# The last expert's down product by column halves: output sums in interleaved quarters

## The reference

```
h2 = rmsnorm(x, ffn_norm_w)
# for each token its top 4 of 32 experts, gates = softmax of their logits
u = h2[tokens of e] @ w_up[e] + b_up[e]          # 1024 -> 2048
glu = min(u[:, 0::2], 7);  lin = clip(u[:, 1::2], -7, 7)
a = glu * sigmoid(1.702 * glu) * (lin + 1)
y = a @ w_down[e] + b_down[e]                    # 1024 -> 1024
x[tokens of e] += gate * y
```

## Time and profile before

| | |
|---|---|
| median of 3 runs | 1147.87 us |
| the three runs | 1146.83, 1147.87, 1149.91 us |
| span of the profiled execution | 1145.4 us |
| TensorE busy | 1097.6 us (96%) |
| VectorE, ScalarE, GpSimd busy | 437.5, 188.0, 88.4 us |
| HBM read, written | 439.78 MB, 2.37 MB |
| mean DMA rate over the span | 386 GB/s |

### The profile page before, as it was taken

The page is one execution under the profiler, slowest core; times in us unless marked ns, Lnnn a source line. Parts: engine busy times, 40 slices in busy tenths (PEclk is TensorE's granted clock), DMA queues, the critical chain, the costliest instruction groups (busy, mean ns, idle before and its releaser), DMA issues.

```text
span 1145.4 us, 15065 instructions
## 1 busy us (share of the span) xinstructions
PE 1097.6 (96%) x6055; PEld 497.1 (43%) x6055; DVE 437.5 (38%) x858; ACT 188.0 (16%) x398; POOL 88.4 (8%) x161
## 2 busy tenths in 40 slices
PE   9999999999999999999898999999999999999997
PEld 6689898543333333333333333333333333333332
DVE  4577786753433223233223232323232323232322
ACT  2133341221321101010101010101010101010101
POOL 1785215000000000000000000000000000000000
PEclk9999999999999999999999999999999999999999
DMA  9947629999999999999999999999999999999997
GB/s 313 314 128 186 210 85 353 416 357 425 400 420 426 419 432 431 430 433 431 433 433 429 434 430 433 435 428 434 429 434 431 431 434 429 435 429 434 425 423 287
DMA packets 53206, 444.36 MB, mean 388 GB/s; under 512 B 13101, under 2 KB 19373, under 8 KB 35741
## 3 DMA queue, kind: packets, MB, share of 16 engines
q1 hardware_dynamic: 46712, 435.83, 91.7%
q0 software_dynamic: 5600, 7.32, 2.4%
q10 hardware_dynamic: 852, 0.64, 0.2%
HBM read 439.78 MB, written 2.37 MB: 386 GB/s over the span
## 4 chain that ended last, share of the span: by engine, by line
PE 62%; DMA 37%; DVE 0%; issue 0%; ACT 0%; ACTq 0%; SPq 0%; DVEq 0%
PE pA L2051 32%; PE pB L2051 21%; DMA ring<-in_w_up 21%; DMA ring<-in_w_down 10%; PE pM L2051 6%; DMA area<-in_w_up 5%; PE pM L2054 1%; PE pA L2054 1%; DMA x<-in_x_prompt 1%; ACT area L1269 0%; DVE x L1898 0%; SPq L800 0%; DVE conv_row L1812 0%; DVE area L1973 0%; DVE x L1978 0%
## 5 line engine op out<-in xcount | busy, mean ns | idle before, releaser
L2051 PE MATMUL pA<-ring,hn 128*64 128x512 f32 x1536 | 352.6, 602 | 23.0 <-DMA ring<-in_w_up 23.0
L2051 PEld LDWEIGHTS pA<-ring,hn 128*64 128x64 f32 x1536 | 105.3, 137 | 218.8 <-issue 185.5
L2051 PE MATMUL pB<-ring,area 128*64 128x512 f32 (+2 forms) x784 | 171.5, 591 | 6.6 <-DMA ring<-in_w_down 5.8
L2051 PE MATMUL pA<-area,hn 128*64 128x512 f32 x512 | 119.3, 610 | 10.4 <-DMA area<-in_w_up 10.4
L2051 PE MATMUL pB<-area,ring 128*128 128x132 f32 (+2 forms) x928 | 126.4, 327 | 0.0
L2051 PEld LDWEIGHTS pB<-area,ring 128*128 128x128 f32 (+1 forms) x928 | 106.7, 175 | 18.2 <-issue 2.3
L2051 PEld LDWEIGHTS pB<-ring,area 128*64 128x64 f32 (+2 forms) x784 | 58.5, 136 | 101.2 <-issue 87.8
L1898 DVE TENSOR_TENSOR x<-pM,x 128x512 f32<-128x512 f32 x60 | 40.1, 691 | 147.7 <-PE pM L2051 147.7
L1257 ACT ACTIVATE area<-area 128x512 f32<-128x512 f32 x30 | 18.9, 631 | 385.2 <-DVE area L1881 385.2
L1812 DVE COPY conv_row<-pM 128x512 f32<-128x512 f32 x30 | 20.6, 686 | 146.0 <-PE pM L2051 146.0
L2051 PEld LDWEIGHTS pA<-area,hn 128*64 128x64 f32 x512 | 36.2, 139 | 74.5 <-issue 59.7
(11 more groups left out here) (348 smaller groups left out, 907.1 us busy)
## 6 DMA issues: line engine op xcount, KB each, us to landing
ring<-in_w_up SPq DMA_DIRECT2D x36, 4096.0 KB, 29.8
ring<-in_w_down SPq DMA_DIRECT2D x18, 4096.0 KB, 29.0
area<-in_w_up SPq DMA_DIRECT2D x12, 4096.0 KB, 30.2
ring<-in_w_up SPq DMA_DIRECT2D x16, 2048.0 KB, 13.4
area<-in_w_down SPq DMA_DIRECT2D x6, 4096.0 KB, 30.0
ring<-in_w_in SPq DMA_DIRECT2D x22, 1024.0 KB, 10.0
ring<-in_w_down SPq DMA_DIRECT2D x16, 1024.0 KB, 11.6
ring<-in_w_up SPq DMA_DIRECT2D x16, 1024.0 KB, 8.4
```

Source lines behind the costliest of these rows:

```text
L2051: return pe.matmul(out, w, m, start=start, stop=stop, skip_group_check=True)
```

## The change

Only the last pair is changed. The four quarters of the 1024 output columns (256 each) are dealt out anew: a = 0 makes quarters 0 and 2, a = 1 quarters 1 and 3. For expert 1 every product of 512 columns becomes two of 256, so that columns 0 to 511 (half 0) collect in one place and columns 512 to 1023 (half 1) in another bank (`last_down`). The last weight row comes in two loads of 512 columns, and half 0 of that row is multiplied as soon as the first is there. `half_done` then lets ScalarE and VectorE copy half 0, and `last_scatter` has a list of six products for each half. The sums of the prompt rows lie so that an addition of VectorE covers two quarters that are not neighbours; the last two stores follow suit. The bias of half 1 is added later, by `last_bias(1)` behind up piece 6. The diff, cut to its core:

```
+        def last_down(a, h):
+            rows_ = slice(64 - 64 * a, 128 - 64 * a)
+            return pA[rows_, 512:768] if h else pB[rows_, 1, 0:256]
+        def last_sums(m, a):
+            if m:
+                return pA[:, 1024 + 512 * a:1536 + 512 * a]
+            return pB[:, 0, :] if a else pA[:, 0:512]
...
+                        if j == 11 and r == ROWS:
+                            cut = SLOT * h + D * (ROWS - 1) + 512
+                            first_half = slice(cut - 512, cut)
+                            sp.dma_start(unit(u)[:, first_half], rows_of(b, PAIRS - 1)[:, first_half]).then_inc(last_half, 16)
+                            f = slice(cut, cut + 512)
...
-                    nc.scalar.activation(y_pair[64:128, 0:512], pB[64:128, 1, :], ACT.Copy).then_inc(y_ready, 1)
+                    act.wait_ge(half_done, 1)
+                    nc.scalar.activation(y_pair[64:128, 0:256], last_down(0, 0), ACT.Copy).then_inc(half_act, 1)
+                    act.wait_ge(down_done, 2 * g + 2)
+                    nc.scalar.activation(y_pair[64:128, 512:768], last_down(0, 1), ACT.Copy).then_inc(y_ready, 1)
...
+                        dve.wait_ge(half_done, 1)
+                        V.tensor_copy(y_pair[0:64, 256:512], last_down(1, 0)).then_inc(half_dve, 1)
                         dve.wait_ge(down_done, 2 * g + 2)
-                        V.tensor_copy(y_pair[0:64, 512:1024], pB[0:64, 1, :]).then_inc(y_ready_dve, 1)
+                        V.tensor_copy(y_pair[0:64, 768:1024], last_down(1, 1)).then_inc(y_ready_dve, 1)
...
+                        if last and (j, r) == (11, ROWS - 1):
+                            for n in range(2):
+                                if n == 0:
+                                    pe.wait_ge(last_half, 16)
+                                else:
+                                    loaded(j, whole=True)
+                                for a in range(2):
+                                    f = slice(D * r + 512 * n + 256 * a, D * r + 512 * n + 256 * a + 256)
+                                    mm = matmul(last_down(a, n), rows_T[:, r, 64 * h:64 * h + 64], w[:, f], start=False)
+                                if n == 0:
+                                    mm.then_inc(half_done, 1)
+                            continue
...
                         for a in range(2):
+                            if last and e == 1:
+                                for n in range(2):
+                                    mm = matmul(last_down(a, n), rows_T[:, r, 64 * h:64 * h + 64],
+                                                w_r[:, 512 * n + 256 * a:512 * n + 256 * a + 256], start=False, stop=False)
...
                 def last_scatter():
+                    for h in range(2):
+                        pe.wait_ge((half_act, y_ready)[h], 1 + g * h)
+                        pe.wait_ge((half_dve, y_ready_dve)[h], 1 + g * h)
+                        for m in (1, 0):
+                            for a in range(2):
+                                rows_ = slice(64 - 64 * a, 128 - 64 * a) if m else slice(0, 128)
+                                f = slice(512 * h + 256 * a, 512 * h + 256 * a + 256)
+                                mm = matmul(last_sums(m, a)[:, 256 * h:256 * h + 256], gate_h[a][rows_, 128 * m:128 * m + 128],
+                                            y_pair[rows_, f], start=(m == 0 and h == 0), stop=(h == 1))
+                                if h:
+                                    mm.then_inc(last_full, 1)
+                        for q in (2 * h, 2 * h + 1):
+                            mm = matmul(b[32 * q:32 * q + 32, 0:256], gate_h[q % 2][:, SEQ:], y_pair[:, 256 * q:256 * q + 256])
                     mm.then_inc(misc_full, 1)
```

More of the change, by code:

```diff
@@ L929, in _ @@
             sp.dma_start(y_prompt[0, 128:256, :], x[:, 1, :]).then_inc(final_stored, 16)
[L930 to L933, removed]
+            for a in range(2):
+                sp.wait_ge(last_dve, 2 + a)
+                sp.dma_start(quarters_of(y_prompt[0, 0:128, :], a), quarters_of(x[:, 0, :], a)).then_inc(final_stored, 16)
             sp.wait_ge(misc_free, MAIN_FILLS)
@@ L2569, in biases, with last_bias @@
                         up_biases(e)
+                    if last and e == 1:
+                        last_bias(0)
+                        return
                     for a in range(2):
+                        if last:
+                            matmul(in_two(pB[y_rows(e, a), e, :]), sel[0:96, e, :],
+                                   quarters_of(bias_down[0:96], a), stop=False)
+                            continue
                         matmul(pB[y_rows(e, a), e, :], sel[0:96, e, :], bias_down[0:96, 512 * a:512 * a + 512],
                                stop=False)
+                def last_bias(h):
+                    for a in range(2):
+                        f = slice(512 * h + 256 * a, 512 * h + 256 * a + 256)
+                        matmul(last_down(a, h), sel[0:96, 1, :], bias_down[0:96, f], stop=False)
                 def act_turn(e, freed=False):
@@ L2599, in down @@
                             w_r = first_down(j, r) if first else w[:, D * r:D * r + D]
+                            if last and e == 1:
+                                for n in range(2):
+                                    mm = matmul(last_down(a, n), rows_T[:, r, 64 * h:64 * h + 64],
+                                                w_r[:, 512 * n + 256 * a:512 * n + 256 * a + 256], start=False, stop=False)
+                                    if freed and r == a == n == 0:
+                                        mm.then_inc(ring_free, 1)
+                                continue
+                            if last:
+                                mm = matmul(in_two(pB[y_rows(e, a), e, :]),
+                                            rows_T[:, r, 64 * h:64 * h + 64], quarters_of(w_r, a),
+                                            start=False, stop=(h == 1 and r == ROWS - 1))
+                                continue
                             mm = matmul(pB[y_rows(e, a), e, :], rows_T[:, r, 64 * h:64 * h + 64], w_r[:, 512 * a:512 * a + 512],
@@ L2661, in first_expert_sums @@
                     pe.wait_ge(y_first, 1)
[L2662 to L2666, removed]
+                    for a in range(2):
+                        s = slice(64 * a, 64 * a + 64)
+                        matmul(in_two(last_sums(1, a)), gate_h[a][s, 128:256], quarters_of(y_pair[s], a),
+                               start=(a == 0), stop=False)
@@ L2668, in last_scatter @@
                 def last_scatter():
                     b = bank(6)
-                    pe.wait_ge(y_ready, g + 1)
-                    pe.wait_ge(y_ready_dve, g + 1)
                     for h in range(2):
-                        s = slice(64 - 64 * h, 128 - 64 * h)
-                        c = 1024 + 512 * h
-                        matmul(pA[:, c:c + 512], gate_h[h][s, 128:256], y_pair[s, 512 * h:512 * h + 512],
-                               start=False).then_inc(last_full, 1)
-                    for h in range(2):
-                        matmul(pA[:, 512 * h:512 * h + 512], gate_h[h][:, 0:128],
-                               y_pair[:, 512 * h:512 * h + 512]).then_inc(last_full, 1)
@@ L2720, in pair @@
                         act_turn(0)
+                    if last:
+                        last_bias(1)
                     if not last:
```

30 lines of the change are left out of this document (20 added, 10 removed).

## The result

The changed kernel takes 1150.37 us (median of 13 runs), the kernel before, in runs taken with them, 1148.23 (13 runs): ratio 1.0019, 95% interval 1.0011 to 1.0026, some 1.3 to 3.0 us slower. By the bound of 0.3% that is no difference; it is on the slow side all the same, and more than the 0.85 us that I had forecast.

What follows compares the result with a forecast made beforehand. Down-weight loads rule until about 1128.0, then TensorE, then the tail, with the stores (DMA) as the end. Profiled span 1145.4 + 0.85 = 1146.25, plus 2.5 us carried over to the median: 1148.7 us, range 1147.0 to 1150.6.

Steps and rivals of the forecast that it cites:

- The last row's load: Expert 1's last weight row loaded in two halves: worth nothing, since TensorE reaches that row at 1135.64 either way.
- The early half: Last row's half 0 done 0.43 us sooner, its copies shorter, so the tail's first sum comes 0.68 us earlier.
- Half 0's list: In the tail, half 0's sums on TensorE run ahead of half 1's and take 2.23 us.
- the sample's share: Sample products within half 0's list of sums on TensorE: 0.55 us of the 2.23.
- The pair and the additions: In the tail, first pair complete and first store issued 1.12 us later; three back-to-back VectorE additions end 0.55 later.
- The stores: Kernel's end: first data at about 1141.4 plus 3.0 us of full DMA, gap closed; end 0.8 us later, 0.85 taken.
- Half the array lags: Rival, expert 1's rows: products start strictly in program order, costing 0.6 us more, 1149.3 us; chance 0.33.
- No overlap: Rival, expert 1's rows: array halves no longer overlap, a row takes 1.28 us or more, 1151.5 to 1154.5 us; chance 0.07.
- Hidden as meant: Rival, tail's sums: second set of fillings and drainings (three of 0.2) isn't paid, change 0, 1147.9 us; chance 0.14.
- dearer rows: Expert 1's 256-column products may cost 0 to 0.5 us more over three rows; 0.5 counted in the range's upper end.
- the spread of a median: Allowance in the range for the measured median: some 0.9 us either way, from runs at 1146.83 to 1149.91.
- Q: Theory from the experiments: SP issues stores one after another; the end follows the last issue by 2.6 to 3.5 us.

Runs made afterwards that it cites:

- e10: Changed kernel with the last weight row loaded whole again, still multiplied and copied in halves; tail 13.79 us, ratio to the kernel before 1.0015.
- e7: Changed kernel with the four sample products behind both lists of sums instead of two in each; tail 14.02 us, ratio to the kernel before 1.0015.
- e3a: Kernel before with its last two prompt stores as quarter pairs (1 KB rows), both issued after the third addition; tail 14.00 us, ratio 1.0005.
- e6: Changed kernel with rows 128 to 255 summed first, sample sums last, column-half stores as before, all prompt stores on SP; tail 12.87 us, ratio to kernel before 1.0005.
- e11: Changed kernel, rows 128 to 255 summed first, column-half stores, the second issued on ScalarE's queue; tail 11.62 us, ratio to the kernel before 1.0005.
- e2: Changed kernel with sums waiting for both halves' copies, in 512-column products, quarter stores kept; tail 13.47 us, ratio to the kernel before 1.0006.
- e4: Changed kernel without SP's two sample stores (half the sample output missing); tail 13.53 us, ratio to the kernel before 1.0015.
- e5: Changed kernel with its second quarter store issued on ScalarE's queue instead of SP's; tail 13.83 us, ratio to the kernel before 1.0008.
- e9: Changed kernel once more, unedited, one run; span 1147.4 us, tail 14.46 us, no ratio.
- e3b: Kernel before with its last two stores, still column halves (2 KB rows), both issued after the third addition; tail 13.81 us, ratio 1.0008.

## Why the prediction was right and where it failed

- **The last row's load: right.** Nothing; e10.
- **The early half: right.** First copy at 3.33 (3.27 by my sum), first sum 0.64 earlier than before (4.53 to 3.89) where I had 0.68.
- **Half 0's list: right.** 2.25 us, predicted 2.23; the sample's share 0.55 by e7, as I had put it, though my sum gives no working for that term.
- **The pair and the additions: right.** First store 1.21 later (1.12 predicted), third addition 0.50 later (0.55). Two additions take 1.33, back to back.
- **The stores: the step that failed.** I wrote that "with the later stores issued sooner behind it the gap closes", and took 0.85 from bounds of 0.55 and 1.22. I counted data, 3.0 us of it, and no issue. The trace that I had showed three issues of SP behind the last addition in 1.15 us (the column store's 0.33, the sample's 0.73); I didn't ask what they would cost as quarters and with nothing between them. What is behind the last addition now takes 2.60 us: 0.64 that is left of the first quarter's 1.21, the second's 0.61, the sample's 1.24, and two gaps of 0.05 to 0.06. So 0.50 to the third addition, 1.45 in issues and 0.43 behind them (0.67 by the second pair of profiles) make the 2.38.
- **Half the array lags: wrong.** In the program a row is a = 0 half 0, a = 0 half 1, a = 1 half 0, a = 1 half 1; the timeline has the four records of pB (both products of half 0) at 1132.36 and the four of pA at 1132.84. So the third product started ahead of the second. By the lag half 0's first copy would have come at 3.87; it comes at 3.33. The strict order that the Trainium skill states (TensorE: Matmul & The Clock Gate, Part 3, The mechanism) is not what these rows show.
- **No overlap: wrong.** It asked for weight rows of 1.28 us; they take 0.86 to 0.91 (1132.36 to 1133.27).
- **Hidden as meant: wrong.** Each new list pays its ends; 2.25 us.

That the range held the time is luck. The sum gave 1148.7, 0.85 us over the kernel before; the measured difference is 2.1 us by the medians and 2.4 to 2.6 by the tails, so the sum was 1.3 to 1.8 us short. 1150.37 lies in the range only because its upper end was drawn for the lag, with 0.5 of dearer rows: neither of the two is there, and 1148.7 with the 0.9 for the spread of a median would have ended at 1149.6.

**Open.** In the four profiles of the kernel before and its two variants the last chunk starts at 1132.60 to 1133.19, in the ten of the changed kernel and its variants at 1132.94 to 1134.66. The loads set it, and it moves by over 1 us between profiles of one kernel (1134.29, 1132.94); whether the change moves it too these runs don't tell. The medians leave little room for it: 2.1 us is no more than the profiles' tails alone differ by.

Why the first quarter's issue takes 1.21 in the changed kernel and 0.67 in e3a, and why a half's takes 1.48 in e6, isn't settled. It is the same in both profiles of the changed kernel, it happens on the queue whose first store is under way, and e11's issue on the other queue escapes it. A quarter's issue tends to take longer, the nearer it starts behind the 512 KB store's: 0.67 at 1.95 us (e3a), 0.92 at 1.09 (e2), 0.88 to 1.32 at 0.63 to 0.64 (the changed kernel, e4, e5, e7, e9, e10). So the data still under way may be what holds the issue, and the issue not the first cause. Column halves don't go by it (0.34 in e6 and e11 and 0.65 in the kernel before at 1.09 to 1.10, but 1.48 in e6 at 1.96), and no run took that store away. A code load that holds an engine meanwhile fits some of them too, and was not taken away in any run either. What lies between the last issue and the end of the span, 2.4 to 3.5 us, is in part data still moving (in the kernel before until about 1143.6, 1.1 us) and has no further account here: it moves by as much as most of the effects above, so the tails bear out Q in direction and in rough size, not to a tenth.

## What to carry to other kernels

At the end of a kernel, price each store as an issue as well as bytes: list the issues of each queue behind the last result, end to end, and see how many fall due at once. Cutting work so that half of it starts earlier helps only the outputs that need that half alone; here every store needed both, so the early half bought a second list of sums and made all stores due together. Try late stores on two queues, and finish first what the largest store needs: the tails of e5 and e11 were 0.6 to 0.9 and 1.25 us shorter than those of the same order on one queue, which the medians don't resolve (1.0008 against 1.0019, and 1.0005 for both e6 and e11).

## What was not expected of the hardware

- An issue of a 256 KB store took 0.33 us at the least in rows of 2 KB (kernel before) and up to 1.48 (e6), in rows of 1 KB 0.61 (changed kernel) to 1.32 (e7); ScalarE's queue, idle in the tail until then, issued one in 0.36 where SP took 1.48 (e11, e6).
- SP's two 8 KB sample stores took 0.73 us in the kernel before and 1.03 to 1.24 in most kernels that issue the stores end to end, but 0.66 in e6 right behind the issue of 1.48; leaving them out shortened the tail by 0.9 to 1.2.
- Loads of code run on the DMA engines beside the last stores: one packet of 16 KB was under way for 1.72 us in e3b, and a remainder of SP's stores came behind it. That it held the kernel's end is not shown.
